# Modulation rows of two layers computed on VectorE beside the feed-forwards, and expert tiles in contiguous runs

## The reference

```python
sc_x, sc_c = silu(c), silu(c_ctx)
for l in range(2):
    mx = (sc_x @ ada_w[l] + ada_b[l]).reshape(bsz, 6, 1, d)   # ada_w[l]: 1024 x 6144
    mc = (sc_c @ ada_w[l] + ada_b[l]).reshape(6, d)
    hx = modulate(rmsnorm(x, norm_g[l, 0]), mx[:, 0], mx[:, 1])
    hc = modulate(rmsnorm(ctx, norm_g[l, 0]), mc[0], mc[1])
    yx, yc = mixer_ab(...) if l == 0 else mixer_mla(...)      # attentions
    x = x + mx[:, 2] * rmsnorm(yx, norm_g[l, 1])
    hx = modulate(rmsnorm(x, norm_g[l, 2]), mx[:, 3], mx[:, 4])
    x = x + mx[:, 5] * rmsnorm(swiglu(hx, ffn_w13[l], ffn_w2[l]), norm_g[l, 3])
    # layer 0 does the same for the context; in layer 1 it is used as keys and values only
# third layer: mixer over x and ctx_2 (scan, gating unit), then 16 experts,
# each on the 32 tokens that score highest for it:
hid = silu(xs @ w_gate) * (xs @ w_up)          # 1024 x 2048 each
ye = (hid @ w_down) * gate                     # 2048 x 1024
```

## Time and profile before

| | us |
|---|---|
| median of 3 runs | 2780.72 |
| lowest, highest | 2779.02, 2782.63 |
| profiled execution, its own time | 2776.35 |
| its span | 2774.4 |
| TensorE busy | 2235.6 (81%) |
| VectorE busy | 576.9 (21%) |
| ScalarE busy | 408.5 (15%) |
| mean rate of all transfers | 221 GB/s |

### The profile page before, as it was taken

The page is one execution under the profiler, slowest core; times in us unless marked ns, Lnnn a source line. Parts: engine busy times, 40 slices in busy tenths (PEclk is TensorE's granted clock), DMA queues, the critical chain, the costliest instruction groups (busy, mean ns, idle before and its releaser), DMA issues.

```text
span 2774.4 us, 25106 instructions
## 1 busy us (share of the span) xinstructions
PE 2235.6 (81%) x10537; PEld 1154.7 (42%) x10537; DVE 576.9 (21%) x1238; ACT 408.5 (15%) x814; POOL 6.2 (0%) x13
## 2 busy tenths in 40 slices
PE   6999988999999899899987789775555555565555
PEld 3444443444444446688834677641111111111111
DVE  3126823000000437200031582310000000000001
ACT  2014533000000325300032122110000000000000
POOL 0000000000000000000000000000000000000000
PEclk9999999999999999999999898987788778778876
DMA  9538841121222210243611231389999999999997
GB/s 367 219 160 307 314 138 61 61 81 42 63 78 68 91 61 31 92 151 103 201 61 61 70 112 70 129 342 418 417 416 417 418 418 418 418 416 416 417 418 300
DMA packets 198800, 613.17 MB, mean 221 GB/s; under 512 B 5360, under 2 KB 98800, under 8 KB 156448
## 3 DMA queue, kind: packets, MB, share of 16 engines
q1 hardware_dynamic: 197824, 608.28, 56.9%
q0 software_dynamic: 864, 3.28, 0.4%
HBM read 610.49 MB, written 1.05 MB: 220 GB/s over the span
## 4 chain that ended last, share of the span: by engine, by line
PE 48%; DMA 31%; DVE 5%; ACT 1%; issue 1%; DVEq 0%; ACTq 0%
PE ps L330 47%; DMA ring<-in_expert_w_up 12%; DMA ring<-in_expert_w_down 12%; DMA ring<-in_expert_w_gate 7%; PE ps L669 1%; DVE AR L635 1%; DVE X L636 1%; DVE AR L1254 0%; DVE AR L1242 0%; DVE AR L1243 0%; ACT H L581 0%; DVE AR L1135 0%; DVE AR L1231 0%; DVE AR L1232 0%; ACT RS L557 0%
## 5 line engine op out<-in xcount | busy, mean ns | idle before, releaser
L330 PE MATMUL ps<-ring,AR 128*32 128x512 f32 (+1 forms) x4096 | 523.2, 659 | 373.9 <-DMA ring<-in_expert_w_up 139.5
L330 PE MATMUL ps<-H,ring 128*128 128x512 f32 (+1 forms) x2416 | 800.5, 493 | 21.1 <-ACT H L581 13.1
L330 PEld LDWEIGHTS ps<-H,ring 128*128 128x128 f32 x2416 | 460.9, 192 | 353.2 <-issue 305.2
L330 PEld LDWEIGHTS ps<-ring,AR 128*32 128x32 f32 x4096 | 144.6, 134 | 735.8 <-issue 257.9
L330 PE MATMUL ps<-AR,ring 128*128 128x256 f32 (+1 forms) x1024 | 299.6, 456 | 3.0 <-DVE AR L793 1.5
L330 PEld LDWEIGHTS ps<-AR,ring 128*128 128x128 f32 x1024 | 196.1, 192 | 106.2 <-issue 84.4
L330 PE MATMUL ps<-AR 128*64 128x128 f32 (+5 forms) x1168 | 213.8, 340 | 29.6 <-DVE AR L1243 9.5
L330 PEld LDWEIGHTS ps<-AR 128*128 128x128 f32 (+2 forms) x1168 | 151.0, 186 | 108.9 <-issue 81.2
L1653 DVE TENSOR_TENSOR AR<-AR,ps 128x512 f32<-128x512 f32 x16 | 11.0, 688 | 590.9 <-PE ps L330 590.9
L793 DVE TENSOR_TENSOR AR<-AR,ps 128x512 f32<-128x512 f32 (+1 forms) x44 | 24.4, 555 | 424.7 <-PE ps L330 424.7
L1639 ACT ACTIVATE AR<-ps 128x512 f32<-128x512 f32 x16 | 9.6, 597 | 548.8 <-PE ps L330 548.8
(11 more groups left out here) (220 smaller groups left out, 1100.3 us busy)
## 6 DMA issues: line engine op xcount, KB each, us to landing
ring<-in_expert_w_gate SPq DMA_DIRECT2D x64, 2048.0 KB, 24.0
ring<-in_expert_w_up SPq DMA_DIRECT2D x64, 2048.0 KB, 23.4
ring<-in_expert_w_down SPq DMA_DIRECT2D x64, 2048.0 KB, 23.9
ring<-in_ada_w SPq DMA_DIRECT2D x36, 2048.0 KB, 8.6
ring<-in_ffn_w SPq DMA_DIRECT2D x44, 1024.0 KB, 7.1
ring<-in_ffn_w SPq DMA_DIRECT2D x16, 1408.0 KB, 7.1
ring<-in_w_in SPq DMA_DIRECT2D x11, 2048.0 KB, 7.9
ring<-in_ab_w_in SPq DMA_DIRECT2D x4, 2048.0 KB, 15.9
```

Source lines behind the costliest of these rows:

```text
L330: m = nc.tensor.matmul(out_, lhsT=lhsT, rhs=rhs, start=start, stop=stop)
```

## The change

Modulation of layers 1 and 2: the 24 jobs leave the first attention. Layer l + 1 is made during feed-forward l as 12 row jobs, each a tile of 512 rows by 1024 columns (4 rows of 4 KB per partition). VectorE multiplies the rows by the condition's element of that partition and adds them up in an accumulator, for two conditions in jobs 0 to 3 (shift and scale of the mixer) and one in the others. After two jobs TensorE sums over the partitions with matmuls against ones, VectorE copies the row out, TensorE transposes it and VectorE puts it into MOD. TensorE waits for each job (`row_done`) before it releases the slot. Expert tiles: partition p gets k consecutive rows, one run of 16 KB, and XS and the transposed hidden state follow that order.

```diff
+        def runs(w, r0, r1):
+            k, n = (r1 - r0) // P, w.shape[-1]
+            return (lambda s: ring[:, s, 0:k * n].rearrange("p (k n) -> p k n", k=k),
+                    w[r0:r1, :].rearrange("(p k) n -> p k n", p=P))
+        def row_job(l, n):
+            w = A["ada_w"][1] if l == 1 else A["ada_w_2"][0]
+            job(("row", l, n), rows(w, n % 2 * 512, (n % 2 + 1) * 512, n // 2 * 1024, (n // 2 + 1) * 1024))
+        def rows_of(i):
+            return (0, 1) if i == 0 else (i + 1,) if i <= 10 else ()
...
                 job(("w13", l, i), ...)
+                for n in rows_of(i):
+                    row_job(l + 1, n)
...
-        ada_jobs(1)
-        ada_jobs(2)
...
-                job(("gu", e, i), rows(w, (i % 4) * 256, (i % 4 + 1) * 256, 0, EF))
+                job(("gu", e, i), runs(w, (i % 4) * 256, (i % 4 + 1) * 256))
-                job(("dn", e, i), rows(A["expert_w_down_2"][0, e], i * 512, (i + 1) * 512, 0, D))
+                job(("dn", e, i), runs(A["expert_w_down_2"][0, e], i * 512, (i + 1) * 512))
...
+        def dve_row_job(c, l, n):
+            if n % 2 == 0 and n:
+                dve_row_copy(c, l, n // 2 - 1)
+            if n % 2 == 1 and n > 1:
+                dve_row_turned(c, l, n // 2 - 1)
+            j = job_at[("row", l, n)]
+            c.eng.wait_ge(slot_loaded[j % SLOTS], loaded_at[j])
+            w = ring[:, j % SLOTS, :].rearrange("p (k n) -> p k n", k=4)
+            acc = row_acc(l, n)
+            conds = 2 if n < 4 else 1
+            for kk in range(4):
+                for cond in range(conds):
+                    by = SC[:, 4 * (n % 2) + kk, l // 2, cond:cond + 1]
+                    if n % 2 + kk == 0:
+                        ins = V.tensor_scalar(acc[:, cond, :], w[:, kk, :], by, None, ALU.mult)
+                    else:
+                        ins = V.scalar_tensor_tensor(out=acc[:, cond, :], in0=w[:, kk, :], scalar=by, in1=acc[:, cond, :],
+                                                     op0=ALU.mult, op1=ALU.add)
+                    if kk == 3 and cond == conds - 1:
+                        c.mark(ins, row_done, 12 * (l - 1) + n + 1)
+                    else:
+                        c.step(ins)
+        def pe_row_job(pe, l, n):
+            if n < 12:
+                pe.wait_ge(row_done.sem, 12 * (l - 1) + n + 1)
+                used()
+            if n % 2 == 1:
+                b = take(pe, ("rows", l, n // 2))
+                acc = row_acc(l, n)
+                conds = 2 if n < 4 else 1
+                for half in range(2):
+                    for cond in range(conds):
+                        j = 32 * (2 * half + cond)
+                        mm(ps[j:j + 32, b, :], ones[:, 0:32], acc[:, cond, half * 512:(half + 1) * 512], True, True,
+                           b if half and cond == conds - 1 else None)
+            elif n:
+                b = take(pe, ("rowsT", l, n // 2 - 1))
+                freed(pe, ("rows", l, n // 2 - 1))
+                for i in range(4):
+                    m = nc.tensor.transpose(ps[:, b, i * P:(i + 1) * P], RS[:, i * P:(i + 1) * P], ident)
+                m.then_inc(bank_full[b], 1)
+        def dve_row_copy(c, l, g):
+            b = full_of(c.eng, ("rows", l, g))
+            if g < 2:
+                c.free(V.tensor_copy(RS[:], ps[:, b, :]), ("rows", l, g))
+            else:
+                c.step(V.tensor_copy(RS[0:32, :], ps[0:32, b, :]))
+                c.free(V.tensor_copy(RS[64:96, :], ps[64:96, b, :]), ("rows", l, g))
...
                     pe_dense(pe, ("g", l, 2 * i + j), w, j * P, H, T, pre=pre if i + j == 0 else None)
+                    for n in rows_of(i - 1)[j:j + 1] if i else ():
+                        pe_row_job(pe, l + 1, n)
                     pe_dense(pe, ("u", l, 2 * i + j), w, 256 + j * P, H, T)
...
             for n in range(KD):
-                pe_dense(pe, (("ffn", l), n), w, 0, hid, T, K=KF)
+                for k in range(KF):
+                    mm(...)
+                    if k == KF // 2 and n < 2:
+                        pe_row_job(pe, l + 1, 11 + n)
...
                 c.free(V.tensor_tensor(hid[:, j, 0:T], TG[:, j % 2, 0:T], ps[:, b, 0:T], ALU.mult), ("u", l, j))
+                if j % 2:
+                    for n in rows_of(j // 2):
+                        dve_row_job(c, l + 1, n)
+            dve_row_copy(c, l + 1, 5)
+            dve_row_turned(c, l + 1, 5)
+            dve_mods(c, l + 1, 0, 2)
+            dve_mods(c, l + 1, 2, 6, 1)
...
-                        mm(ps[:, b, k * P:(k + 1) * P], HTOK[:, t, (4 * half + k) * P:(4 * half + k + 1) * P],
+                        mm(ps[:, b, k * P:(k + 1) * P], HTOK[:, t, (2 * half + k // 2) * 256 + k % 2:(2 * half + k // 2 + 1) * 256:2],
...
-                    m = nc.tensor.transpose(ps[:, b, i * P:(i + 1) * P], HS[:, i * P:(i + 1) * P], ident)
+                    m = nc.tensor.transpose(ps[:, b, i * P:(i + 1) * P], HS[:, i::4], ident)
...
-        attn0 = Attention(ab_units, pe_ada_beside, dve_ada_beside)
+        attn0 = Attention(ab_units)
...
-            for l in (1, 2):
-                dve_mods(c, l)
```

More of the change, by code:

```diff
@@ L222, in build @@
         late_loaded = sem("late_loaded")
+        row_done = Signal(sem("row_done"))
         exp_ready = sem("exp_ready")
@@ L256, in rows, with ada_jobs @@
                     w[r0:r1, c0:c1].rearrange("(k p) n -> p k n", p=P))
-        def ada_jobs(l, which=range(12)):
-            w = A["ada_w_2"][0] if l == 2 else A["ada_w"][l]
+        def runs(w, r0, r1):
+            k, n = (r1 - r0) // P, w.shape[-1]
+            return (lambda s: ring[:, s, 0:k * n].rearrange("p (k n) -> p k n", k=k),
+                    w[r0:r1, :].rearrange("(p k) n -> p k n", p=P))
+        def ada_jobs(l, which):
+            w = A["ada_w"][l]
             for i in which:
@@ L481, in dve_ada_turned, with dve_mods @@
             c.free(V.tensor_copy(dst, src), ("adaT", l, g))
-        def dve_mods(c, l, lo=0, hi=6):
+        def dve_mods(c, l, lo, hi, conds=2):
             n = 8 * (hi - lo)
-            bias = vec(f"ada_b{l}", 8 * lo, n).unsqueeze(2).broadcast_to([P, n, 2])
-            c.step(V.tensor_tensor(MOD[:, l, 8 * lo:8 * hi, :], MOD[:, l, 8 * lo:8 * hi, :], bias, ALU.add))
+            cs = slice(0, conds)
+            bias = vec(f"ada_b{l}", 8 * lo, n).unsqueeze(2).broadcast_to([P, n, conds])
+            c.step(V.tensor_tensor(MOD[:, l, 8 * lo:8 * hi, cs], MOD[:, l, 8 * lo:8 * hi, cs], bias, ALU.add))
             for w in range(2):
@@ L489, in dve_mods @@
                     g = vec("norm_g", (l * 4 + 2 * w) * 8, 8) if l < 2 else vec(("norm_mix", "norm_ffn")[w], 0, 8)
-                    c.step(V.scalar_tensor_tensor(out=AMP[:, l, w, :, :], in0=MOD[:, l, 24 * w + 8:24 * w + 16, :],
-                                                  scalar=1.0, in1=g.unsqueeze(2).broadcast_to([P, 8, 2]),
+                    c.step(V.scalar_tensor_tensor(out=AMP[:, l, w, :, cs], in0=MOD[:, l, 24 * w + 8:24 * w + 16, cs],
+                                                  scalar=1.0, in1=g.unsqueeze(2).broadcast_to([P, 8, conds]),
                                                   op0=ALU.add, op1=ALU.mult))
                 if l < 2 and lo <= 3 * w + 2 < hi:
-                    g = vec("norm_g", (l * 4 + 2 * w + 1) * 8, 8).unsqueeze(2).broadcast_to([P, 8, 2])
-                    c.step(V.tensor_tensor(GATE[:, l, w, :, :], MOD[:, l, 24 * w + 16:24 * w + 24, :], g, ALU.mult))
+                    g = vec("norm_g", (l * 4 + 2 * w + 1) * 8, 8).unsqueeze(2).broadcast_to([P, 8, conds])
+                    c.step(V.tensor_tensor(GATE[:, l, w, :, cs], MOD[:, l, 24 * w + 16:24 * w + 24, cs], g, ALU.mult))
         def pe_adaln0(pe):
@@ L506, in dve_adaln0, with row_acc @@
             dve_mods(c, 0, 0, 2)
[L511 to L524, removed]
+        def row_acc(l, n):
+            both = n < 4
+            at = 13056 if l == 2 else 13312 if both else 13824
+            return ar(at, 2 if both else 1, 1024)
@@ new lines, in dve_row_copy, with dve_row_turned @@
+        def dve_row_copy(c, l, g):
[5 more added lines that the diff above has]
+                c.free(V.tensor_copy(RS[64:96, :], ps[64:96, b, :]), ("rows", l, g))
+        def dve_row_turned(c, l, g):
+            b = full_of(c.eng, ("rowsT", l, g))
+            conds = 2 if g < 2 else 1
+            src = ps[:, b, :].rearrange("p (i h c s) -> p h i c s", i=4, h=2, c=2)[:, :, :, 0:conds, 0]
+            dst = MOD[:, l, 8 * g:8 * g + 8, 0:conds].rearrange("p (h i) c -> p h i c", h=2)
+            c.free(V.tensor_copy(dst, src), ("rowsT", l, g))
@@ L776, in pe_ffn @@
                 w = weights(pe, ("w2", l, n))[:, 0:KF * P].rearrange("p (k n) -> p k n", k=KF)
-                pe_dense(pe, (("ffn", l), n), w, 0, hid, T, K=KF)
+                b = take(pe, (("ffn", l), n))
+                for k in range(KF):
+                    mm(ps[:, b, 0:T], w[:, k, :], hid[:, k, 0:T], k == 0, k == KF - 1, b if k == KF - 1 else None)
```

(8 more changed lines are left out.)

## The result

| | before | after |
|---|---|---|
| median, us (4 runs each) | 2779.87 | 2849.12 |
| lowest, highest | 2777.32, 2782.63 | 2848.77, 2850.95 |
| profiled execution, its span | 2776.35, 2774.4 | 2848.84, 2846.9 |

The ratio is 1.025 (95% interval 1.0233 to 1.0268): 69 us slower. The direction was forecast, but with 39 us; the time lies above the stated range.

The account below looks back on a forecast made before the run. TensorE was taken to bound the first attention and feed-forwards, VectorE the kind-b units, transfers the experts. Attention -28, feed-forwards +86 and experts -19 sum to 39 us more, from 2779 to 2818; 2799 to 2842 leaves 2 in 10 out.

Parts of the forecast that it names:

- First attention: Stage before the output projection: taking the 24 modulation jobs out saves 28 us, bounds 18 and 33.
- VectorE binds: First attention, kind-a units: without the jobs VectorE sets the pace, 2.41 us a unit where the period is 3.19.
- the 1.00 of kind b: First attention's second stretch: clock stayed 1.00 with TensorE idle 3.5 of 42.1 us, read as frequent waits not dropping it.
- Price of a row job: VectorE in the feed-forwards: 1285 ns per 1024-column scalar_tensor_tensor, about 0.75 us per opening tensor_scalar.
- Waits: Feed-forwards 0 and 1: TensorE waits for VectorE's row jobs, 13.3 and 47.8 us in all.
- New work on TensorE: Each feed-forward: six sets of summing matmuls and six sets of four transposes, together 9.5 us a layer.
- Clock in the feed-forwards: Long waits for row jobs drop TensorE to 1.2 GHz: 1.5 us in feed-forward 0, 5 us in feed-forward 1.
- rival D: Feed-forward 1: the clock also falls after the waits of jobs 4 to 10, 17 us, total 2835; 10%.
- Experts: Last third, bound by transfers: 16 KB runs save 19 us, bounds 46 saved and 11 lost; tiles near 425 GB/s.
- sums of 14 and 46: Experts' saving in us by two piece costs: 14 from gate/up against down windows, 46 from the feed-forwards' 1 KB pieces.
- E: First attention gives 10 us less since the loop through ScalarE binds, total 2828; 10%.

Follow-up runs that it names:

- att_empty: The kernel before without the 24 modulation jobs of layers 1 and 2, their transfers, transposes and copies: 2779.29 us, ratio 0.9999.
- att_fill4: As att_empty, with four filler matmuls on TensorE after every second unit of the first attention: 2761.55 us, ratio 0.9925 against the kernel before.
- ffn_quarter: The changed kernel with VectorE doing only the first of the four rows of each row job: 2771.19 us, ratio 0.9955 against the kernel before.
- ffn_late: The changed kernel with TensorE's wait for a row job one gate and one up group later: 2778.76 us, ratio 0.9989 against the kernel before.
- after_mended: The changed kernel with the late wait of ffn_late and the filler of att_fill4: 2764.62 us, ratio 0.9945 against the kernel before.

## Why the prediction was wrong, by its steps

**First attention, forecast -28, measured -6.4** (and -7.6 to +1.5 in the other kernels without jobs there). This step failed. "VectorE binds" was right where the clock was full: 9.96 us for four units against the 9.6 of the forecast. Wrong was the assumption that TensorE's prices in the earlier trace rows stay when its load goes. I weighed the clock only where TensorE waits long, and took the 1.00 of kind b as a sign that short waits are harmless. The jobs, which I counted as a cost on TensorE, also kept its clock; att_empty and att_fill4 show it, 359.9 us without and 348.8 with filler. With the clock kept the gain is 18.6 us by att_fill4, still not 28; its filler has its own price. Four units take 10.7 us with it against 9.6, which over the 32 units of kind a makes some 9 us (an estimate from these two numbers).

**Price of a row job.** Right: 1285 ns and 753 ns.

**Waits, forecast 13.3 and 47.8 us, measured 13.1 and 43.9.** Right, job by job but for two: job 1 waited 1.3 instead of 3.7 us, since the matmuls in its cover ran at the slow clock (32 records in 9.31 us, forecast 6.83), and job 11 did not wait, where 1.0 was forecast. The parts of the first sum make 13.1, not 13.3.

**New work on TensorE, forecast 9.5 us a layer.** ffn_quarter has 9.6 and 11.1 more than before. Right.

**Clock in the feed-forwards, forecast 1.5 and 5, measured 8 and 12** (what the stages lost, 30.9 and 67.4, less the waits and the new work as ffn_quarter has it; 6 and 10 of it in the gate and up matmuls). The mechanism was right, this term of the sum was too small by factors of five and two and a half. In feed-forward 0 all three waits dropped the clock, where the sum had 1.5 out of 7 us. In feed-forward 1 three of the seven waits for jobs 4 to 10 dropped it too, at 1.7 us each: the 48 records behind the job 8 wait took 12.06 us, those behind the job 6 wait 10.38. That is 5 of the 17 us of rival D; the three long waits make the other 7, for which 5 had been taken. The Trainium skill (TensorE: Matmul & The Clock Gate, "HAM oscillation — how this bites in real kernels") names the effect for bursts split by recurring waits, and the trace agrees for the feed-forwards, 0.94 in the second. For the first attention, where no wait over kind a is longer than 1.2 us, that section gives no drop; the measured 0.71 decides.

**Experts, forecast -19, measured -19.9 in the profiles.** Right, with 428 GB/s against the 425 named, and partly luck: 19 was chosen between sums of 14 and 46. The bounds held. The ceiling of 435 GB/s that the Trainium skill gives (DMA: Bandwidth & Descriptors, "Where 436 GB/s comes from") was not passed. The same section of the Trainium skill says that transfers between HBM and SBUF are bound at about 358 GB/s; the measured 428, with one core running, decides otherwise.

Of the 33 us between forecast and the spans' difference, 22 lie in the attention and 12 in the feed-forwards; the experts gave 1 back. With the attention's miss alone the forecast would have been 2840, inside the range; it took both. Every rival missed the time. E had part of the attention's gain lost, but to the loop; none had it lost for a reason that lies in the removed work.

Open: why the part behind feed-forward 1 is 4 us longer in the three kernels that leave the modulation out (1389.7 to 1390.1 against 1385.4), and why the same attention starts its projection anywhere from 359.8 to 368.9 us. I tried nothing on either.

## What to carry to other kernels

Work taken off TensorE need not be paid back at the old price, for its clock can fall with it, as here: before counting such a gain, ask whether the stage keeps 2.4 GHz without it, and test by leaving the work out with nothing put in its place, and again with filler. When an in-order engine must wait for another, sum the other's job against the work that stands between, for every job; two thirds of the feed-forwards' loss (67 of 98 us) went by moving one call by two groups of matmuls. Bind two independent edits only after each is timed: the contiguous runs alone were worth some 20 us (24 between the medians) and were hidden in a loss of 69.

## What the runs showed of the hardware that was not expected

TensorE fell to 1.2 GHz for spells like the 15.4 us above in a stage in which it waited 1.2 us at most; in the fast stretch before such a spell it was busy for 8.58 of 10.00 us. Four filler matmuls after every second unit kept the granted clock at 0.98, two kept it at 0.97. Three kernels whose clock swings there vary more from run to run: att_empty 2772.4 to 2791.7 us in 8 runs, ffn_quarter 2759.1 to 2779.3 in 8 and ffn_late 2769.3 to 2789.2 in 10, against 2776.4 to 2785.6 in 19 of the kernel before and 2763.5 to 2766.5 in 4 of after_mended. The changed kernel doesn't fit this: with a clock of 0.71 there its 4 runs lie within 2.2 us, so the link isn't shown. Runs of 16 KB per partition moved 428 GB/s where those of 4 and 8 KB made 417 over the same 750 us.
